# Retention: the first sequence's state one step later, and half of the first head's output weights split in step 0

## The chip, the cores and the metric

One NeuronCore of a Trainium2 chip runs the whole program. The metric is the device time of one execution in microseconds (us); the number compared is the median over several runs.

## The reference, cut to what matters

One step of a two-layer decoder for a prompt of 1024 tokens and 8 sample sequences of 8 tokens. The second layer is retention, and the change lies in it and in its output projection. Per head (4 of them, keys of 256, values of 512), with chunks of 128 tokens for the prompt and of 8 tokens for the samples:

```python
def step(S, inp):
    qc, kc, vc = inp
    o_inter = jnp.einsum('bhtk,bhkv->bhtv', qc, S) * q_decay
    scores = jnp.einsum('bhtk,bhsk->bhts', qc, kc) * intra_decay[None]
    o_intra = jnp.einsum('bhts,bhsv->bhtv', scores, vc)
    S_new = chunk_decay * S + jnp.einsum('bhsk,bhsv->bhkv', kc * k_decay, vc)
    return S_new, o_inter + o_intra
...
o = rms_norm(o).reshape(b, t, W_C) * jax.nn.silu(g.astype(f32))
return o.astype(h.dtype) @ w_out, s_new
```

A sample sequence is one such chunk: its output is computed from its old state `s0`, and its new state is `gamma^8 * s0 + k^T v` over its 8 tokens.

## The kernel before, in words

`retention_out` is the last stage of the program. Its main loop has `NSTEP = 32` steps, 4 heads by 8 prompt chunks, and every engine runs through the same steps by a program of its own; semaphores alone tie them together. Nothing is scheduled by a tool: the order of an engine's instructions is the order of the code.

In step n TensorE (the `block.tensor` program, `pe`) does, in this order:

1. the output of chunk n into `o`: three products of split operands (L2555), and from the second chunk of a head on the products with the running state (L2560), which wait for `state_done` of step n-1;
2. the update of the state into `u[0]`, `u[1]` (`product` at L2569); it waits until `s1_done` says that the sample state last put into `u` has been read;
3. `scores(n + 2)`, which needs that chunk's `q` and `k` in SBUF (`qk_in`);
4. `turn_out`, the transposes of the normed and gated output of step n-1;
5. in steps 2, 6, ... `sample_outputs`, the outputs of four sample sequences;
6. `sample_states(n - 1)`, the update of one sample sequence's state: two matmuls (L2505) into `u[0]` and `u[1]`;
7. `product_out`, the output projection of chunk n-2: 24 matmuls (L2528) with the weights `w_hi`, `w_lo`;
8. in steps 3, 7, ... the transposes of the sample outputs.

The sample keys and values are split into a high and a low part once, and then their rows are stacked by small SBUF to SBUF transfers, 8 partitions each: `stack(seq)` on ScalarE's queue writes three pieces of `v_stack`, `stack_keys(seq)` on GpSimd's queue three of `k_stack`. `sample_states(m)` waits for both (`stacked[m]`, `stacked_k[m]`). ScalarE stacks sequence n+1 in step n, GpSimd stacks sequence n in step n.

VectorE adds the state updates (L2772, L2775), gates (L2712), makes the low parts, writes the new sample states `s1` from `s0` and `u` (L2733), and adds the projection to the residual `y` (L2747). ScalarE rounds to the high parts and norms. The weights of a head's projection come as four rows `r` of 128 x 1024: `round_weights` on ScalarE makes `w_hi`, and `split_weights` makes `w_lo`, rows 0 and 2 on VectorE, rows 1 and 3 on GpSimd. For head 0 ScalarE does that in step 1, VectorE in step 1, GpSimd in step 3 of its own count.

SyncE (`sp`) issues the loads and stores on one queue, in the order of its code. In step n: `q`, `k` of chunk n+3, `v` of chunk n+3, the gate rows `g` of chunk n+3 (after `gated` of step n), then the store of the sample state n-1 (after `s1_done`), loads of later sample states into `s0`, and one tile of `y`. What stands behind a wait of this program is issued late.

Of the kernel before, what the change touches and what calls it, by code (L numbers as in the profile page):

```python
# [2174 lines left out]
def retention_out(nc, ahead, q_fm, k_fm, v_tm, g_tm, state_in, state_prompt, state_samples, mix_fm, consts, weight, x_of, y_of):  # L2175
# [6 lines left out]
    with nc.cleanup_on_exit(), ExitStack() as ctx:  # L2182
# [3 lines left out]
        NCH, J, R = TP // P, DK // P, DV // P  # L2186
        NGRP, SEQS = 2, NS // 2
        ROWS = SEQS * LS
        NSTEP = HC * NCH
# [87 lines left out]
        def outs_in(n):  # L2277

            return [] if n < 2 else [x for x in outs if x[0] == (n - 2) // NCH and x[1] == (n - 2) % NCH or
                                     (n - 2) % NCH == 6 and x == ((n - 2) // NCH, NT - 1)]  # L2280

        def qd_until(n):

            return n - n // NCH
# [14 lines left out]
        @block.sync  # L2299
        def _(sp):  # L2300
            def load_qk(n):
                h, c = divmod(n, NCH)
                for dst, src in ((q, q_cols), (k, k_cols)):
                    sp.dma_start(dst[:, n % NQ], src[h, :, c]).then_inc(qk_in[n % NQ], 16)

            def load_v(n):
                h, c = divmod(n, NCH)
                sp.dma_start(v[:, n % NV], v_rows[c * P:c * P + P, h]).then_inc(v_in[n % NV], 16)

            def load_g(n):  # L2310
                h, c = divmod(n, NCH)
                sp.dma_start(g[:, n % NV], g_rows[c * P:c * P + P, h]).then_inc(g_in[n % NV], 16)

            def load_s0(n):
                h, c = divmod(n, NCH)
                sp.dma_start(s0[c % SEQS][:], state_in[c, h].rearrange("(j k) v -> k j v", k=P)).then_inc(s0_in[c % SEQS], 16)

            def load_gs(h, grp):
                at = TP + grp * ROWS
                for s in range(SEQS):  # L2320
                    sp.dma_start(g_s[s * ROWS:(s + 1) * ROWS, grp, :], g_rows[at:at + ROWS, h]).then_inc(gs_in[grp], 16)

            def load_raw(h):
                for r in range(0 if h else 2, R):
                    sp.dma_start(raw_of(h, r), w_rows[:, h * R + r, :]).then_inc(raw_in[r], 16)

            def load_y(t):
                sp.dma_start(y[t][0:rows_of(t)], x_of(t)).then_inc(y_in[t], 16)

            def store_samples(m):  # L2330
                h, c = divmod(m, NCH)
                sp.wait_ge(s1_done, J * (m + 1))
                sp.dma_start(state_samples[c, h].rearrange("(j k) v -> k j v", k=P), s1[m % 2]).then_inc(s1_left[m % 2], 16)

            for x in ahead.left_tm:
                sp.wait_ge(x, LEFT)
            load_g(0)
            load_s0(0)
            load_g(1)
            for n in range(NSTEP):  # L2340
                h, c = divmod(n, NCH)
                if n + NQ < NSTEP:
                    sp.wait_ge(kt_done, n + 1)
                    sp.wait_ge(qd_done, qd_until(n))
                    load_qk(n + NQ)
                if n + NV < NSTEP:
                    sp.wait_ge(v_split, n + 1)
                    load_v(n + NV)
                    if n == 0:
                        load_raw(0)  # L2350
                        load_g(2)
                        for x in range(1, SEQS):
                            load_s0(x)
                        load_gs(0, 0)
                    sp.wait_ge(gated, unit_of["step", n] + 1)
                    load_g(n + NV)
                if c == NCH - 1:
                    sp.wait_ge(state_done, J * (n + 1))
                    sp.dma_start(state_prompt[h].rearrange("(j k) v -> k j v", k=P), state[:]).then_inc(state_left, 16)
                if n:  # L2360
                    store_samples(n - 1)
                    if (n - 1) % SEQS and n + 3 < NSTEP:
                        sp.wait_ge(o_done, unit_of["samples", (n - 1) // SEQS] + 1)
                        for x in (n + 2, n + 3) if (n - 1) % SEQS == 1 else (n + 3,):
                            load_s0(x)
                if 1 <= n < NCH:
                    if n == 4:
                        sp.wait_ge(w_split_d, R // 2)
                        sp.wait_ge(w_split_p, R // 2)
                    load_y(n - 1)  # L2370
                if n == 2:
                    load_gs(0, 1)
                if n == NCH - 1:
                    for seq in range(NS):
                        sp.wait_ge(stacked[seq], NSTACK)
                        sp.wait_ge(stacked_k[seq], NSTACK)
                    load_y(NT - 1)
                    load_y(NT - 2)
                if n % SEQS == 3 and h + 1 < HC:
                    sp.wait_ge(gated, unit_of["samples", n // SEQS] + 1)  # L2380
                    load_gs(h + 1, n // SEQS % NGRP)
                if c == NCH - 1 and h + 1 < HC:
                    sp.wait_ge(w_split_d, R // 2 * (h + 1))
                    sp.wait_ge(w_split_p, R // 2 * (h + 1))
                    load_raw(h + 1)
            store_samples(NSTEP - 1)
            for h, t in outs[-NT:]:
                sp.wait_ge(added, 2 * out_of[h, t] + 2)
                sp.dma_start(y_of(t), y[t][0:rows_of(t)]).then_inc(y_left, 16)
            sp.wait_ge(state_left, 16 * HC)  # L2390
            for i in range(2):
                sp.wait_ge(s1_left[i], 16 * NSTEP // 2)
            sp.wait_ge(y_left, 16 * NT)

        @block.gpsimd
        def _(pool):
            def split_weights(h):
                for r in range(1, R, 2):
                    pool.wait_ge(w_rounded, R * h + r + 1)
                    nc.gpsimd.tensor_tensor(w_lo[:, r, :], raw_of(h, r), w_hi[:, r, :].bitcast(F32), ALU.subtract).then_inc(w_split_p, 1)  # L2400

# [18 lines left out]
            for n in range(NSTEP):  # L2420
# [15 lines left out]
                        nc.gpsimd.tensor_copy(pick[:, s * LS:s * LS + LS], ident[:, at:at + LS]).then_inc(picked, 1)  # L2436
                elif n < NS:
                    stack_keys(n)
                if n == 3:
                    split_weights(0)  # L2440
                if n >= NCH and (n - 2) % NCH == 1 and n > NCH + 2:
                    split_weights((n - 3) // NCH)

# [1 line left out]
        def _(pe):  # L2445
# [44 lines left out]
                                       stop=(j == J - 1), skip_group_check=True, tile_position=(0, s * ROWS))  # L2490
                mm.then_inc(o_done, 1)

            def sample_states(m):


                h, c = divmod(m, NCH)
                if m < NCH:
                    pe.wait_ge(stacked[m], NSTACK)
                    pe.wait_ge(stacked_k[m], NSTACK)
                grp, rows = c // SEQS, slice(c % SEQS * ROWS, c % SEQS * ROWS + 3 * LS)  # L2500
                for j in range(J):
                    pe.wait_ge(state_done, J * min(m + 1, NSTEP - 1) + j + 1)
                    if m == NSTEP - 1:
                        pe.wait_ge(s1_done, J * (m - 1) + j + 1)
                    pe.matmul(u[j][:], k_stack[rows, grp, h, j], v_stack[rows, grp, h], start=True, stop=True,  # L2505
                              tile_position=(c % SEQS * ROWS, 0)).then_inc(us_done, 1)
# [40 lines left out]
            for n in range(NSTEP):  # L2547
# [16 lines left out]
                if n == 0:  # L2564
                    pe.wait_ge(first_scm, 1)
                for j in range(J):
                    if n >= 2:
                        pe.wait_ge(s1_done, J * (n - 2) + j + 1)
                    product(u[j][:], (kd_hi[:, i, j], kd_lo[:, i, j]), values).then_inc(u_done, 1)  # L2569

                if n + 2 < NSTEP:
# [7 lines left out]
                        pe.wait_ge(first_qd, 1)  # L2579
                    sample_outputs(h, c // SEQS)  # L2580

                if n:
                    sample_states(n - 1)
                for x in outs_in(n):
                    product_out(*x)
                for x in samples_before:
                    pe.wait_ge(picked, SEQS)
                    turn_out(x)
            sample_states(NSTEP - 1)
            for n in range(NSTEP, NSTEP + 2):  # L2590
                for x in turned_in(n) if n == NSTEP else ():
                    turn_out(x)
# [4 lines left out]
        def _(act):  # L2597
# [37 lines left out]
                act.wait_ge(tr_done, m + 1)  # L2635
                nc.scalar.copy(hi, src).then_inc(m_rounded, 1)

            def round_weights(h):
                for r in range(R):
                    if h and r < R - 1:  # L2640
                        act.wait_ge(w_used, (R - 1) * (h - 1) + r + 1)
                    elif h:
# [24 lines left out]
            for n in range(NSTEP):  # L2667
# [4 lines left out]
                    stack(n + 1)  # L2672
                for m in turned_in(n):
                    round_mix(m)
                if n == 1:
                    round_weights(0)
                if n % SEQS == 2:
                    norm(unit_of["samples", n // SEQS])
                if n > NCH and n % NCH == 1:
# [5 lines left out]
        def _(dve):  # L2685
# [30 lines left out]
                dve.wait_ge(m_rounded, m + 1)  # L2716
                dve.tensor_tensor(lo, src, hi.bitcast(F32), ALU.subtract).then_inc(m_split, 1)

            def split_weights(h):
                for r in range(0, R, 2):  # L2720
                    dve.wait_ge(w_rounded, R * h + r + 1)
                    dve.tensor_tensor(w_lo[:, r, :], raw_of(h, r), w_hi[:, r, :].bitcast(F32), ALU.subtract).then_inc(w_split_d, 1)

# [41 lines left out]
            for n in range(NSTEP):  # L2765
# [14 lines left out]
                step_before, *samples_before = turned_in(n) or [None]  # L2780
                if n:
                    split_mix(step_before)
                if n:
                    sample_states(n - 1)
                if n == 1:
                    split_weights(0)
                if n % SEQS == 2:
                    gate(unit_of["samples", n // SEQS])
                for x in outs_in(n):
                    add(*x)  # L2790
                for m in samples_before:
                    split_mix(m)
                if n > NCH and n % NCH == 1:
# [141 lines left out]
```

## Time and profile before

| | us |
|---|---|
| median of 3 runs | 2029.87 |
| the three runs | 2022.57, 2029.87, 2030.99 |
| the profiled execution, its own time | 2025.5 |
| its span, first to last instruction | 2023.5 |
| TensorE matmul busy, whole span | 1877.1 (93%) |
| VectorE, ScalarE, GpSimd busy | 852.8, 520.0, 594.4 |

The busy shares are averages over stages. The stage of this change begins near 1600 us and ends with the program; the profiled execution is 2.0 us longer than its span, and what happens in that stage is read from the rows further down. "PE" is TensorE's matmul side, "PEld" its weight load, "DVE" VectorE, "ACT" ScalarE, "POOL" GpSimd, "SP" SyncE; a "q" behind a name is that engine's DMA queue.

### The profile page before, as it was taken

Reading aid. Unit: us, or ns where it says so; the run is one execution under the profiler, and the core shown is the slowest. Engines: PE = TensorE matmul, PEld = TensorE weight load, DVE = VectorE, ACT = ScalarE, POOL = GpSimd, SP = SyncE. Lnnn points to the kernel's source line nnn. Section 1 sums busy time; section 2 is a strip of 40 time slices with the busy share of each in tenths; the row PEclk is TensorE's granted clock in tenths of the full one; section 3 lists DMA queues with packets and bytes.
Section 4 is the critical chain, followed back from the end, with each engine's and each line's share of the span. In section 5 each row is a group of like instructions: output and inputs, shape, how many; then the busy total and the mean of one; then the engine's idle time right before and its main releaser. Section 6 shows DMA issues by size and latency. Waiting matters only on the chain. (4 is left out here: it accounts for less than half of the span.)

```text
span 2023.5 us, 30854 instructions
## 1 busy us (share of the span) xinstructions
PE 1877.1 (93%) x11538; PEld 1511.4 (75%) x11538; DVE 852.8 (42%) x1474; ACT 520.0 (26%) x1133; POOL 594.4 (29%) x532
## 2 busy tenths in 40 slices
PE   6999999988887885789999999999999889999998
PEld 5788999974454553667899998888888657777776
DVE  3552000038788445874344442111000255656564
ACT  5210111047676432343310000000111232323231
POOL 3333222026666004313052222233330141313120
PEclk9999999989899897798999999999999989999999
DMA  4233224141330675345433223222324487665643
GB/s 154 78 107 107 99 103 139 50 141 46 118 115 27 207 224 192 115 133 175 132 122 90 86 86 101 89 91 93 101 95 128 124 226 249 193 199 155 203 136 141
DMA packets 209993, 261.58 MB, mean 129 GB/s; under 512 B 24260, under 2 KB 150660, under 8 KB 209604
## 3 DMA queue, kind: packets, MB, share of 16 engines
q1 hardware_dynamic: 154756, 201.50, 31.9%
q10 hardware_dynamic: 53104, 53.04, 8.0%
q0 software_dynamic: 2000, 5.25, 0.9%
q8 instruction: 86, 1.41, 0.3%
q14 instruction: 47, 0.39, 0.1%
HBM read 175.97 MB, written 81.40 MB: 127 GB/s over the span
## 5 line engine op out<-in xcount | busy, mean ns | idle before, releaser
L476 PE MATMUL odd_bank<-odd_w_hi,odd_h_hi 128*128 128x512 f32 x576 | 224.1, 389 | 0.0
L476 PE MATMUL odd_bank<-odd_w_lo,odd_h_hi 128*128 128x512 f32 x576 | 224.1, 389 | 0.0
L476 PE MATMUL odd_bank<-odd_w_hi,odd_h_lo 128*128 128x512 f32 x512 | 199.2, 389 | 0.0
L419 POOL CAST odd_w_hi<-ahead_raw 128x1024 fp32r<-128x1024 f32 x48 | 51.5, 1073 | 332.9 <-PE odd_bank L476 312.2
L476 PE MATMUL odd_bank<-odd_h_hi,odd_w_hi 128*128 128x362 f32 (+1 forms) x384 | 126.0, 328 | 1.8 <-POOL odd_w_lo L421 1.8
L476 PE MATMUL odd_bank<-odd_h_lo,odd_w_hi 128*128 128x362 f32 (+1 forms) x384 | 126.0, 328 | 0.0
L476 PE MATMUL even_bank<-even_h_hi,even_w_lo 128*128 128x362 f32 (+1 forms) x384 | 126.0, 328 | 0.0
L476 PE MATMUL even_bank<-even_h_hi,even_w_hi 128*128 128x362 f32 (+1 forms) x384 | 125.9, 328 | 0.0
L476 PE MATMUL even_bank<-even_h_lo,even_w_hi 128*128 128x362 f32 (+1 forms) x384 | 125.8, 328 | 0.0
L476 PE MATMUL odd_bank<-odd_h_hi,odd_w_lo 128*128 128x362 f32 (+1 forms) x384 | 125.0, 326 | 0.0
L476 PEld LDWEIGHTS odd_bank<-odd_w_lo,odd_h_hi 128*128 128x128 f32 x576 | 108.1, 188 | 22.4
L476 PEld LDWEIGHTS odd_bank<-odd_w_hi,odd_h_hi 128*128 128x128 f32 x576 | 108.1, 188 | 22.4
L476 PE MATMUL even_bank<-even_w_hi,even_h_hi 128*128 128x512 f32 x288 | 113.9, 395 | 5.0 <-DVE even_head_n L842 4.4
L421 POOL TENSOR_TENSOR odd_w_lo<-ahead_raw,odd_w_hi 128x1024 fp32r<-128x1024 f32 x48 | 115.9, 2414 | 3.8
L476 PE MATMUL even_bank<-even_w_lo,even_h_hi 128*128 128x512 f32 x288 | 113.0, 392 | 0.0
L476 PEld LDWEIGHTS odd_bank<-odd_w_hi,odd_h_lo 128*128 128x128 f32 x512 | 96.1, 188 | 20.0
L2528 PE MATMUL rt_y<-rt_w_hi,rt_m_hi 128*128 128x512 f32 x256 | 103.3, 404 | 0.0
L419 POOL CAST even_w_hi<-even_raw 128x1024 fp32r<-128x1024 f32 x32 | 33.6, 1050 | 232.3 <-PE even_bank L476 192.3
L476 PE MATMUL even_bank<-even_w_hi,even_h_lo 128*128 128x512 f32 x256 | 100.6, 393 | 0.0
L660 ACT ACT_TABLE_LOAD x2 | 2.6, 1283 | 380.3 <-PE odd_bank L476 380.3
L2528 PE MATMUL rt_y<-rt_w_hi,rt_m_lo 128*128 128x512 f32 x256 | 100.0, 391 | 0.0
L2528 PE MATMUL rt_y<-rt_w_lo,rt_m_hi 128*128 128x512 f32 x256 | 99.7, 390 | 0.0
(349 smaller groups left out, 4099.7 us busy)
## 6 DMA issues: line engine op xcount, KB each, us to landing
ahead_raw<-in_w_in_odd SPq DMA_DIRECT2D x48, 512.0 KB, 3.7
even_raw<-in_w_in_even SPq DMA_DIRECT2D x32, 512.0 KB, 3.9
k_page<-in_cache_k SPq DMA_DIRECT2D x64, 256.0 KB, 3.0
v_page<-in_cache_v SPq DMA_DIRECT2D x64, 256.0 KB, 3.0
rt_s<-in_state_ret SPq DMA_DIRECT2D x32, 512.0 KB, 5.4
v_tm<-odd_shared ACTq DMA_DIRECT2D x64, 128.0 KB, 1.9
g_tm<-odd_shared ACTq DMA_DIRECT2D x64, 128.0 KB, 1.9
first_place<-v_tm SPq DMA_DIRECT2D x32, 256.0 KB, 5.2
```

The source lines that it names most:

```text
L419: nc.gpsimd.tensor_copy(hi, r).then_inc(w_hi_done, 1)
L421: nc.gpsimd.tensor_tensor(lo, r, hi.bitcast(F32), ALU.subtract).then_inc(w_split, 1)
L476: mm = pe.matmul(out, stationary, moving, start=(j == 0), stop=(j == len(pairs) - 1))
L660: nc.scalar.activation(stage_tm[0:r, slot, :], src[0:r, :], ACT.Silu).then_inc(freed[0], 1)
L2528: mm = pe.matmul(yp[half][:], a[:, r, :], b[:, r, cols], start=(r == 0 and j == 0), stop=(r == R - 1 and j == len(ops) - 1))
```

## The change

A new table `states_in(n)` says whose sample state is computed in step n: none in steps 0 and 1, sequence 0 in step 2, sequences 1 and 2 in step 3, and from step 4 on sequence n-1 as before. TensorE's and VectorE's `sample_states` and SyncE's stores and `s0` loads follow it. In step 3 the second sequence comes behind `product_out`. The first head's weights are rounded and split in two halves: rows 0 and 1 in step 0 and rows 2 and 3 in step 1 on ScalarE, row 0 in step 0 and row 2 in step 1 on VectorE, row 1 in step 2 and row 3 in step 3 on GpSimd.

```diff
+        def states_in(n):
+            return {0: [], 1: [], 2: [0], 3: [1, 2]}.get(n, [n - 1])
...
-                if n:
-                    store_samples(n - 1)
-                    if (n - 1) % SEQS and n + 3 < NSTEP:
-                        sp.wait_ge(o_done, unit_of["samples", (n - 1) // SEQS] + 1)
-                        for x in (n + 2, n + 3) if (n - 1) % SEQS == 1 else (n + 3,):
+                for m in states_in(n):
+                    store_samples(m)
+                    if (m % SEQS or n == 2) and m + SEQS < NSTEP:
+                        sp.wait_ge(o_done, unit_of["samples", m // SEQS] + 1)
+                        for x in (m + SEQS - 1, m + SEQS) if m % SEQS == 1 and n > 3 else (m + SEQS,):
                             load_s0(x)
...
-                if n == 3:
-                    split_weights(0)
+                if n in (2, 3):
+                    split_weights(0, (2 * n - 3,))
...
-                    pe.wait_ge(state_done, J * min(m + 1, NSTEP - 1) + j + 1)
-                    if m == NSTEP - 1:
+                    pe.wait_ge(state_done, J * min(n, NSTEP - 1) + j + 1)
+                    if m != states_in(n)[0] or n == NSTEP:
                         pe.wait_ge(s1_done, J * (m - 1) + j + 1)
...
-                    if n >= 2:
-                        pe.wait_ge(s1_done, J * (n - 2) + j + 1)
+                    if n >= 3:
+                        pe.wait_ge(s1_done, J * states_in(n - 1)[-1] + j + 1)
...
-                if n:
-                    sample_states(n - 1)
+                behind, *more_behind = states_in(n) or [None]
+                if n >= 2:
+                    sample_states(behind, n)
                 for x in outs_in(n):
                     product_out(*x)
+                for x in more_behind:
+                    sample_states(x, n)
...
-                if n == 1:
-                    round_weights(0)
+                if n < 2:
+                    round_weights(0, (2 * n, 2 * n + 1))
...
-                if n:
-                    sample_states(n - 1)
-                if n == 1:
-                    split_weights(0)
+                behind, *more_behind = states_in(n) or [None]
+                if n >= 2:
+                    sample_states(behind)
+                if n < 2:
+                    split_weights(0, (2 * n,))
                 if n % SEQS == 2:
                     gate(unit_of["samples", n // SEQS])
                 for x in outs_in(n):
                     add(*x)
+                for m in more_behind:
+                    sample_states(m)
```

The order of the instructions, at three places. First TensorE at the border from step 1 to step 2 of the main loop; line numbers differ by a few between the two kernels. Before:

```order
L2459 MATMUL rt_sckt<-first_place 128x128 x2
L2461 MATMUL rt_sckt<-first_place 128x128 x2
L2472 MATMUL rt_tr<-first_place,rt_og 128x128 x4
L2505 MATMUL rt_u<-rt_v_stack,rt_k_stack 128x512 x2
L2451 MATMUL rt_o<-rt_v_hi,rt_scm_hi 128x512
```

and of the change:

```order
L2465 MATMUL rt_sckt<-first_place 128x128 x2
L2467 MATMUL rt_sckt<-first_place 128x128 x2
L2478 MATMUL rt_tr<-first_place,rt_og 128x128 x4
L2457 MATMUL rt_o<-rt_v_hi,rt_scm_hi 128x512
L2457 MATMUL rt_o<-rt_v_lo,rt_scm_hi 128x512
```

The two matmuls of the sample state, which need the stacked rows, no longer stand between the transposes of step 1 and the products of step 2.

Second VectorE over steps 0 and 1, from the low part of the scores of chunk 2 on. Before:

```order
L2701 TENSOR_TENSOR rt_scm_lo<-first_place,rt_scm_hi 128x128
L2775 SCALAR_TENSOR_TENSOR rt_state<-rt_state,rt_u 128x512 x2
L2712 SCALAR_TENSOR_TENSOR rt_og<-rt_o,rt_rs,rt_g 128x512
L2693 TENSOR_TENSOR first_place<-rt_sckt,first_place 128x128
L2698 SCALAR_TENSOR_TENSOR rt_kd_lo<-rt_sckt,ahead_k_dec,rt_kd_hi 128x256
L2701 TENSOR_TENSOR rt_scm_lo<-first_place,rt_scm_hi 128x128
L2717 TENSOR_TENSOR rt_m_lo<-rt_tr,rt_m_hi 128x512
L2733 SCALAR_TENSOR_TENSOR rt_s<-rt_s,rt_u 128x512 x2
L2722 TENSOR_TENSOR rt_w_lo<-ahead_raw,rt_w_hi 128x1024
L2722 TENSOR_TENSOR rt_w_lo<-rt_y,rt_w_hi 128x1024
```

and of the change:

```order
L2710 TENSOR_TENSOR rt_scm_lo<-first_place,rt_scm_hi 128x128
L2731 TENSOR_TENSOR rt_w_lo<-ahead_raw,rt_w_hi 128x1024
L2784 SCALAR_TENSOR_TENSOR rt_state<-rt_state,rt_u 128x512 x2
L2721 SCALAR_TENSOR_TENSOR rt_og<-rt_o,rt_rs,rt_g 128x512
L2702 TENSOR_TENSOR first_place<-rt_sckt,first_place 128x128
L2707 SCALAR_TENSOR_TENSOR rt_kd_lo<-rt_sckt,ahead_k_dec,rt_kd_hi 128x256
L2710 TENSOR_TENSOR rt_scm_lo<-first_place,rt_scm_hi 128x128
L2726 TENSOR_TENSOR rt_m_lo<-rt_tr,rt_m_hi 128x512
L2731 TENSOR_TENSOR rt_w_lo<-rt_y,rt_w_hi 128x1024
```

The first weight row's low part now stands ahead of the state update of step 1, and the sample state (L2733) is gone from step 1.

Third SyncE's queue from the `q` of chunk 4 (step 1) to the `q` of chunk 5 (step 2). Before:

```order
L2304 DMA first_place<-q_fm 128x256
L2304 DMA first_place<-k_fm 128x256
L2308 DMA first_place<-v_tm 128x512
L2312 DMA rt_g<-g_tm 128x512
L2333 DMA out_ret_sample<-rt_s 128x2x512
L2328 DMA rt_y<-y 128x1024
L2304 DMA first_place<-q_fm 128x256
```

and of the change:

```order
L2309 DMA first_place<-q_fm 128x256
L2309 DMA first_place<-k_fm 128x256
L2313 DMA first_place<-v_tm 128x512
L2317 DMA rt_g<-g_tm 128x512
L2333 DMA rt_y<-y 128x1024
L2309 DMA first_place<-q_fm 128x256
```

The store of the first sample state, which waits for `s1_done`, moves from step 1 to step 2, behind the loads of chunk 5.

## Rows read from the trace of the kernel before

**Rows 1.** The profile page's first line: span of the execution.

```profile
span 2023.5 us, 30854 instructions
```

**Rows 2.** What TensorE waited for, 1600 to 2023 us: total, times, longest.

```profile
PE rt_u L2505 <- issue: 7.7, 1, 7.7
PE rt_sckt L2459 <- PEq L219: 3.3, 1, 3.3
...
PE rt_tr L2472 <- DVE rt_ms L2717: 0.2, 1, 0.2
```

**Rows 3.** Windows: length, busy of PE, PEld, DVE, ACT, POOL, clock, DMA, GB/s.

```profile
1638.00:1658.00 20.00, 20.00 (x89) 15.14 (x90) 9.98 (x18) 4.37 (x13) 3.52 (x5) 1.00 0.72 199
...
1950.00:2000.00 50.00, 50.00 (x229) 35.67 (x228) 26.97 (x46) 11.77 (x34) 4.64 (x5) 1.00 0.30 98
```

**Rows 4.** TensorE's timeline, steps 1 and 2: start, length, group, [idle before].

```profile
1613.97 1.95 PE L2560 MATMUL rt_o<-rt_state,ahead_place 128*128 128x512 f32 x4 [0.58 <-DVE rt_state L2772]
1615.36 0.79 PE L2451 MATMUL rt_u<-rt_v_hi,rt_kd_hi 128*128 128x512 f32 x1
...
1617.15 0.61 PE L2459 MATMUL rt_sckt<-first_place 128*128 128x128 f32 x4
...
1617.81 0.60 PE L2472 MATMUL rt_tr<-first_place,rt_og 128*128 128x128 f32 x4
1626.12 1.19 PE L2505 MATMUL rt_u<-rt_v_stack,rt_k_stack 24*128 24x512 f32 x2 [7.71 <-issue]
1627.24 0.80 PE L2451 MATMUL rt_o<-rt_v_hi,rt_scm_hi 128*128 128x512 f32 x1
...
1628.69 2.90 PE L2560 MATMUL rt_o<-rt_state,ahead_place 128*128 128x512 f32 x4
1631.02 0.80 PE L2451 MATMUL rt_u<-rt_v_hi,rt_kd_hi 128*128 128x512 f32 x1
...
1633.70 0.71 PE L2459 MATMUL rt_sckt<-first_place 128*128 128x128 f32 x4 [0.71 <-DMA first_place<-k_fm]
...
1637.84 0.73 PE L2505 MATMUL rt_u<-rt_v_stack,rt_k_stack 24*128 24x512 f32 x2
1638.49 0.50 PE L2528 MATMUL rt_y<-rt_w_hi,rt_m_hi 128*128 128x512 f32 x1
```

**Rows 5.** DMA issues 1616 to 1620 us: count, KB each, us to landing.

```profile
first_place<-v_tm SPq DMA_DIRECT2D x1, 256.0 KB, 17.3
rt_v_stack<-rt_raw ACTq DMA_DIRECT2D x3, 64.0 KB
...
first_place<-k_fm SPq DMA_DIRECT2D x1, 128.0 KB, 17.0
```

**Rows 6.** SyncE's queue in time, steps 1 and 2.

```profile
1616.67 0.43 SPq L2304 DMA_DIRECT2D first_place<-k_fm  x1
...
1628.31 0.40 SPq L2333 DMA_DIRECT2D out_ret_sample<-rt_s  x1
```

**Rows 7.** ScalarE, VectorE and GpSimd in time, steps 0 to 2.

```profile
1618.16 0.60 ACT L2622 ACTIVATE rt_og<-rt_o 128x512 f32<-128x512 f32 x1 [1.93 <-issue]
...
1624.13 1.99 ACT L2645 CAST rt_w_hi<-ahead_raw 128x1024 fp32r<-128x1024 f32 x2
...
1617.27 1.27 DVE L2775 SCALAR_TENSOR_TENSOR rt_state<-rt_state,rt_u 128x512 f32<-128x512 f32 x2
...
1628.20 1.47 DVE L2722 TENSOR_TENSOR rt_w_lo<-ahead_raw,rt_w_hi 128x1024 fp32r<-128x1024 f32 x1
...
1618.82 1.26 POOL L2417 TENSOR_TENSOR rt_v_lo<-first_place,rt_v_hi 128x512 fp32r<-128x512 f32 x1
```

**Rows 8.** Windows of 2 us, columns as in rows 3.

```profile
1620.00:1622.00 2.00, 0.00 (x0) 0.00 (x0) 1.16 (x4) 0.66 (x2) 1.99 (x5) 0.62 1.13 260
...
1626.00:1628.00 2.00, 1.88 (x4) 1.16 (x5) 1.00 (x2) 2.00 (x3) 1.79 (x1) 0.50 0.61 167
...
1630.00:1632.00 2.00, 2.00 (x6) 1.01 (x5) 2.00 (x1) 0.38 (x1) 1.88 (x1) 0.82 1.00 273
```

More of the change, by code:

```diff
@@ L2396, in _, with split_weights @@
         def _(pool):
-            def split_weights(h):
-                for r in range(1, R, 2):
+            def split_weights(h, rows=(1, 3)):
+                for r in rows:
                     pool.wait_ge(w_rounded, R * h + r + 1)
@@ L2491, in sample_outputs, with sample_states @@
                 mm.then_inc(o_done, 1)
-            def sample_states(m):
+            def sample_states(m, n):
                 h, c = divmod(m, NCH)
@@ L2588, in _ @@
                     turn_out(x)
-            sample_states(NSTEP - 1)
+            sample_states(NSTEP - 1, NSTEP)
             for n in range(NSTEP, NSTEP + 2):
@@ L2636, in round_mix, with round_weights @@
                 nc.scalar.copy(hi, src).then_inc(m_rounded, 1)
-            def round_weights(h):
-                for r in range(R):
+            def round_weights(h, rows=range(R)):
+                for r in rows:
                     if h and r < R - 1:
@@ L2717, in split_mix, with split_weights @@
                 dve.tensor_tensor(lo, src, hi.bitcast(F32), ALU.subtract).then_inc(m_split, 1)
-            def split_weights(h):
-                for r in range(0, R, 2):
+            def split_weights(h, rows=(0, 2)):
+                for r in rows:
                     dve.wait_ge(w_rounded, R * h + r + 1)
```

## The prediction

> **What bounds the kernel now.** I read four views, from the coarse to the fine. The list of waits over the last stage first: from 1600 us on TensorE waits once for long, 7.7 us, at the first sample state's matmul (L2505); the next in the list is the stage's start-up, 3.3, and the last 0.2 us [rows 2]. Then the windows: from 1638 us on TensorE is busy for the whole of each stretch, 20.00 of 20 us and still 50.00 of 50 at 1950, at the full clock [rows 3]. So the end of the program is the moment at which the steady state begins plus a fixed amount of TensorE work. I take as that moment the first `product_out`, at 1638.49 us [rows 4]. Whatever the change does after it, on engines that have half their time free, costs or gives nothing as long as TensorE stays full. All of the question is what stands between 1617.81 and 1638.49.
>
> Third, TensorE's timeline there [rows 4]. Its transposes of step 1 begin at 1617.81. Then it is idle for 7.71 us and resumes at 1626.12 with the sample state. The running state that this matmul also waits for was ready at 1617.27 + 1.27 = 1618.54 [rows 7], so what is late are the stacked rows, which come by small transfers. From 1626.12 it works up to the scores of chunk 4, and there it waits again, 0.71 us, for `k` of chunk 4, and starts at 1633.70. The fourth view is the DMA list: `k` was issued at 1616.67 [rows 6] and took 17.0 us [rows 5], so it landed at 1633.7. `v` of the same chunk took 17.3 us. This is the point of the case: the second wait is short only because the first one stands before it. Both belong to one backlog of transfers, issued at the head of the stage, that drains until about 1634.
>
> **The change part by part.**
>
> *The sample state leaves step 1.* TensorE goes from the transposes of step 1 straight to the products of step 2. They need the low part of `v`, ready at 1618.82 + 1.26 = 1620.08 [rows 7]. The state products behind them need the running state of step 1. That one now stands behind a new instruction on VectorE: the low part of weight row 0, which needs ScalarE's rounding of it. ScalarE does two rows in 1.99 us and begins at 1618.16, where the norm of step 1 began [rows 7]; the first row is done at about 1619.2. VectorE's part takes 1.47, which gives 1620.7, and the state update another 1.27: 1622.0 in place of 1618.54. The three products ahead take 1.45 us even at the half clock (1627.24 to 1628.69) [rows 4], from 1620.1 to 1621.5, so TensorE waits half a microsecond here. The state products take 2.33 us at the half clock (1628.69 to 1631.02) or 1.39 at the full one (1613.97 to 1615.36), the products into `u` 1.79 at the full clock (1615.36 to 1617.15) [rows 4]; at the half clock I take 1.7 times that, 3.0. So TensorE comes to the scores of chunk 4 between 1622.0 + 1.39 + 1.79 = 1625.2 and 1622.0 + 2.33 + 3.0 = 1627.3, 6.4 to 8.5 us earlier than now.
>
> *What is late next.* Exactly `k` of chunk 4. SyncE issues it ahead of everything that the change moves: the order shows `q`, `k`, `v`, `g` of that step in the same places, and only behind them the first tile of `y` and the loads of chunk 5 in place of the store of the sample state. So it is issued at 1616.67 as before, and its 17 us are queueing behind what was issued earlier. Two things change around it. ScalarE's stacking of sequence 2 moves behind the two roundings, some 2 us later, and GpSimd's stacking of sequence 3 behind a weight split; that takes traffic out of the way. And `y` (512 KB) with `q`, `k`, `v` of chunk 5 (512 KB) come in at about 1623 in place of 1628; that adds traffic, but later in the same queue. No row of before shows how the landing answers to either. From below: if the stackings that moved had been all that held it, it would come about 2 us earlier, by their shift; if all of the backlog went, the wait would vanish and only the 6.4 to 8.5 us above bound the gain. From above: 1 MB of new traffic at what such stretches move (260 GB/s in the row at 1620, 273 at 1630 [rows 8]) is about 3.8 us, if `k` had to wait for all of it. I take 1 us earlier, 1632.7, nearer to no change than to either end, because the issue time and everything ahead of it in its own queue stay.
>
> The Trainium skill bears on this (DMA: Bandwidth & Descriptors, section on queues, rings and completion order): each of the 16 DMA engines takes the descriptors of one queue in ring order and goes round the queues by packet; and its section on the semaphore increment by 16 says that a copy of 8 partitions runs on 8 engines alone, the lowest-numbered. By that rule the 8-partition stackings load half of the engines, and `k` ends with the slower half; the trace agrees in that the mean DMA share is 0.61 from 1626 to 1628 while `k` is still outstanding [rows 8]. By ring order alone the landing would stay at 1633.7, and the sum below would be 1 us larger, 2028.0 in place of 2027.0, inside the forecast's own case.
>
> *The clock.* Now TensorE is idle from 1618.4 to 1626.1, and its granted clock falls to half, 1.2 GHz, in the row at 1620 (0.62) and is there still in the row at 1626 (0.50). In the row from 1630 to 1632 it is 0.82, so half for 2 * 0.18 / 0.5 = 0.7 us and full, 2.4 GHz, from about 1630.7, 4.6 us after work resumed [rows 8]. Today these 4.6 us cost nothing, since the 0.71 us of waiting for `k` follows. After the change the long idle time, about 1626 to 1632.7, stands directly before the piece that nothing absorbs: scores, transposes, sample outputs, sample state, up to the projection. At the full clock that piece takes 1638.49 - 1633.70 = 4.79 us. At the half clock the sample state took 1.12 (1626.12 to 1627.24) against 0.65 (1637.84 to 1638.49), and the state products 2.33 against 1.39, a ratio of 1.7 in both [rows 4]. 4.6 us at that ratio do the work of 2.7, a loss of 1.9 us. From below the loss is nothing, should the burst at 1620 to 1626 keep the clock up; from above 2.4, were the whole piece slow and it recovered no sooner than the piece ends.
>
> *The sample state that is still owed.* Before, states 0 and 1 are done ahead of the first projection, after it only state 0 is; the third one in step 3 is the missing one. It now falls in the full stretch: 0.65 us [rows 4].
>
> *Weights, `s0` loads, stores.* The weight rows are all ready before the projection at 1638 in both orders: row 3 is rounded by about 1629 and split in 2 to 3.5 us on GpSimd. In step 3 the state of sequence 2 comes behind the projection on TensorE and VectorE, and the `u` products of step 4 wait for VectorE to read it. Between them TensorE has 8 small transposes and the output products, over 2.5 us, against two VectorE instructions; that is hidden, and if it were not, it would cost at most 1 us once. Loads of `s0` go out one step apart and are needed three steps later. All of this I cost at nothing.
>
> **The sum:** -1.0 (landing) + 1.9 (clock) + 0.65 (owed state) = +1.5 us. The profiled execution took 2025.5 us, so 2027.0; its span of 2023.5 [rows 1] grows by the same. The median shown is 4.4 us above that execution, and from it the sum would be 2031.4. The three runs lie from 2022.57 to 2030.99, so I set the forecast between the two, 2029.0. Since 0.5% is 10 us and that is about what a measurement of this kernel can tell from no change, the forecast is no change.
>
> **Rivals.**
>
> *The stall moves to `k` of chunk 4 and the time stays* (forecast), 0.78. By the bounds of the landing and the clock, -2.0 + 0 + 0.65 = -1.4 to 0 + 2.4 + 0.65 = +3.1.
>
> *The gain is kept.* Loads land much earlier since the stackings are spread, and TensorE finds `k` there at 1625.2 to 1627.3. For it: the stackings share the DMA engines with `k`, and ACT's three of 64 KB each stand in the same list [rows 5]. Against it: most of what is ahead of `k` in its own queue is not touched. Price: -8.5 + 0.65 = -7.9 to -6.4 + 0.65 = -5.8 us; from a base of 2029.0 - 1.5 = 2027.5 that is 2019.6 to 2021.7. Even whole it is 0.39%. Chance 0.14, with the part-way cases.
>
> *The loads collide and it gets slower.* `y` and chunk 5 enter the DMA engines five microseconds earlier and take bandwidth from `k`: landing at 1637.5, and +3.8 + 2.4 + 0.65 = +6.9 us, 2034.4. It speaks for it that the DMA share is near 1 in the windows at 1620 and 1630 [rows 8], against it that they stand behind `k`. It would be slower by over 0.5% only if the landing came 7.1 us later than now, past 1640.8. Chance 0.08.
>
> **How the numbers follow.** No case by itself crosses 10 us in either direction; what crosses it is the scatter of the runs, 8.4 us over three. So faster 0.05, within 0.5% 0.90, slower 0.05. The range takes the lowest run less 1.4 and the highest plus 4.5, part of the way into the two rivals: 2021.0 to 2035.5.
>
> **What would show it.** Right, if in the new profile the 7.7 us at L2505 are gone and a wait of 5 to 8 us stands before the scores of chunk 4, released by the DMA of `k_fm`, with the clock at half behind it, and the first projection begins between 1637 and 1642. The step on the landing is wrong if that wait is under 4 us or `k` lands before 1630; the step on the clock is wrong if the granted clock is full through the sample outputs. The forecast as a whole is wrong if TensorE has gaps after the first projection, which I costed at nothing.

## The result and the profile after

The change is slower: its median over 9 runs is 2034.22 us (2031.01 to 2039.52), that of the kernel before over 9 runs beside it 2029.87 (2022.57 to 2038.1); the ratio is 1.0042, 95% interval 1.0024 to 1.0060. That is 5 to 12 us, clear of zero, and the interval reaches over the 0.5% that I had called no change. The ratio compares runs of the same rounds; the two medians by themselves are 4.4 us apart. The profiled execution took 2031.74 us, with a span of 2030.0.

```profile
span 2030.0 us, 30855 instructions
```

The list of waits of TensorE over the last stage of the change (total, times, longest):

```profile
PE rt_sckt L2465 <- DMA first_place<-k_fm: 11.3, 2, 10.7
PE rt_sckt L2465 <- PEq L219: 3.3, 1, 3.3
...
PE rt_o L2457 <- issue: 1.8, 1, 1.8
PE rt_o L2566 <- DVE rt_state L2784: 1.4, 1, 1.4
```

The 7.7 us at the sample state of [rows 2] are gone, and 10.7 us before the scores of chunk 4 have come. TensorE's timeline of the change shows what follows them, beside [rows 4]:

```profile
1613.78 0.60 PE L2478 MATMUL rt_tr<-first_place,rt_og 128*128 128x128 f32 x4
1616.14 0.47 PE L2457 MATMUL rt_o<-rt_v_hi,rt_scm_hi 128*128 128x512 f32 x1 [1.77 <-issue]
...
1618.47 1.95 PE L2566 MATMUL rt_o<-rt_state,ahead_place 128*128 128x512 f32 x4 [1.40 <-DVE rt_state L2784]
...
1632.54 1.23 PE L2465 MATMUL rt_sckt<-first_place 128*128 128x128 f32 x4 [10.74 <-DMA first_place<-k_fm]
...
1634.97 1.93 PE L2491 MATMUL rt_o<-first_place,rt_scm_s 32*32 32x512 f32 x8
1636.84 3.54 PE L2495 MATMUL rt_o<-rt_s,ahead_place 128*32 128x512 f32 x16
1640.30 0.73 PE L2511 MATMUL rt_u<-rt_v_stack,rt_k_stack 24*128 24x512 f32 x2
1640.96 0.50 PE L2534 MATMUL rt_y<-rt_w_hi,rt_m_hi 128*128 128x512 f32 x1
```

The absolute times of two executions can't be set against each other here: this stage began at 1598.23 us in the change's profile and at 1601.67 in that of before, by chance of what lies ahead of it. From here on every time of this stage is counted from the stage's first matmul. So counted, the scores of chunk 4 begin at 1632.54 - 1598.23 = 34.3 in place of 32.0, the first projection (the `product_out` of step 2) at 42.7 in place of 36.8, and from the projection to the end it is 2030.0 - 1640.96 = 389.0 in place of 2023.5 - 1638.49 = 385.0. The three differences, 2.3 (wait), 3.6 (from the scores to the projection, 8.4 in place of 4.8) and 4.0 (after it), make 9.8 us.

The windows of the change (length, busy of PE, PEld, DVE, ACT, POOL, clock, DMA, GB/s) show the clock of the middle piece, and a second dip:

```profile
1624.00:1626.00 2.00, 0.00 (x0) 0.00 (x0) 2.00 (x4) 1.30 (x5) 1.71 (x1) 1.00 1.16 233
1626.00:1628.00 2.00, 0.00 (x0) 0.00 (x0) 0.38 (x1) 0.00 (x0) 0.73 (x1) 0.62 0.78 101
1632.00:1636.00 4.00, 3.46 (x18) 2.30 (x18) 0.97 (x3) 1.28 (x3) 3.15 (x5) 0.50 0.37 129
1636.00:1640.00 4.00, 4.00 (x24) 0.60 (x16) 0.69 (x1) 0.58 (x1) 0.33 (x1) 0.50 0.44 75
1640.00:1642.00 2.00, 2.00 (x11) 1.16 (x8) 1.09 (x2) 1.19 (x4) 0.00 (x0) 0.97 0.00 0
...
1660.00:1664.00 4.00, 4.00 (x10) 2.16 (x9) 1.19 (x3) 0.27 (x1) 0.00 (x0) 0.58 0.93 316
```

TensorE had been idle since 1621.8, and the clock fell to half in the row that begins at 1626 (0.62). Work resumed at 1632.54, and the clock was at 1.2 GHz (0.50) until about 1640.1 (0.97 in the row that begins at 1640), 7.6 us; in [rows 8] it had come back 4.6 us after work resumed. It fell to half once more in step 3, from 1660.6 on, with TensorE busy throughout; there the same state products that took 1.88 us one step earlier took 3.39:

```profile
1647.22 1.88 PE L2566 MATMUL rt_o<-rt_state,ahead_place 128*128 128x512 f32 x4
...
1658.15 1.06 PE L2511 MATMUL rt_u<-rt_v_stack,rt_k_stack 24*128 24x512 f32 x2 [0.23 <-DVE ahead_place L2742]
1659.14 1.08 PE L2480 MATMUL rt_tr<-rt_pick,rt_og 128*128 128x32 f32 x8
...
1660.99 3.39 PE L2566 MATMUL rt_o<-rt_state,ahead_place 128*128 128x512 f32 x4
```

On SyncE's queue `k` of chunk 4 goes out as early in the stage as before (14.7 us after its first matmul, before 15.0), and the new traffic is there, 5 us and more ahead of [rows 6]:

```profile
1612.90 1.09 SPq L2309 DMA_DIRECT2D first_place<-k_fm  x1
...
1619.39 0.43 SPq L2333 DMA_DIRECT2D rt_y<-y  x1
1619.92 0.38 SPq L2309 DMA_DIRECT2D first_place<-q_fm  x1
```

### The profile page after: what moved, and what is told of

The parts are those of the page before. It is cut to its first block and busy times, and to the rows that moved or that the text cites. A ratio compares the mean times of both kernels' runs of the same rounds, so it can differ in the third digit from the quotient of the medians.

```text
span 2030.0 us, 30855 instructions
## 1 busy us (share of the span) xinstructions
PE 1875.3 (92%) x11538; PEld 1508.7 (74%) x11538; DVE 852.7 (42%) x1474; ACT 519.8 (26%) x1133; POOL 592.8 (29%) x532
```

## The experiments

All ratios are to the kernel before, timed in the same rounds, with 95% intervals. "One run" means that the kernel was only profiled. The table gives, from one profile of each, the start of the scores of chunk 4, the start of the first projection (both from the stage's first matmul), the time from that projection to the end of the program, and the sum of the last two, in us (each rounded by itself).

| run | ratio | scores 4 | projection | to the end | sum |
|---|---|---|---|---|---|
| the kernel before | 1 | 32.0 | 36.8 | 385.0 | 421.9 |
| before_again | one run | 31.6 | 36.4 | 385.0 | 421.5 |
| the change | 1.0042 (1.0024 to 1.0060) | 34.3 | 42.7 | 389.0 | 431.7 |
| change_again | 1.0034 (1.0014 to 1.0055) | 34.5 | 42.8 | 388.1 | 430.9 |
| states_only | 1.0033 (1.0012 to 1.0055) | 32.7 | 41.7 | 388.9 | 430.6 |
| weights_only | 0.9987 (0.9970 to 1.0005) | 31.4 | 36.2 | 385.0 | 421.2 |
| hold_loads | 1.0015 (0.9995 to 1.0035) | 29.6 | 38.6 | 388.4 | 427.0 |
| pair_in_2 | 1.0039 (1.0020 to 1.0058) | 32.6 | 41.7 | 387.9 | 429.5 |
| warm | 1.0014 (0.9995 to 1.0033) | 34.0 | 38.7 | 389.1 | 427.8 |
| hold_warm | 0.9992 (0.9967 to 1.0017) | 29.4 | 34.2 | 386.5 | 420.7 |
| hold_before | one run | 33.1 | 42.1 | 388.1 | 430.2 |
| k_first | 0.9985 (0.9963 to 1.0007) | 25.4 | 30.1 | 387.1 | 417.2 |
| k_first_again | 0.9983 (0.9959 to 1.0007) | 23.5 | 38.0 | 389.4 | 427.5 |
| k_first_before | 0.9975 (0.9952 to 0.9997) | 29.8 | 36.9 | 385.6 | 422.4 |
| k_first_old_weights | 1.0000 (0.9970 to 1.0030) | 21.8 | 32.7 | 389.0 | 421.7 |
| k_first_pair | 0.9969 (0.9945 to 0.9992) | 26.4 | 31.1 | 386.4 | 417.4 |
| k_first_pair_again | 1.0001 (0.9979 to 1.0024) | 23.6 | 29.7 | 390.7 | 420.4 |

**1. Which half of the change costs.** states_only keeps the states' new place and takes the weights back to where they were; weights_only is the reverse.

```diff
 # states_only, against the change
...
-                if n < 2:
-                    round_weights(0, (2 * n, 2 * n + 1))
+                if n == 1:
+                    round_weights(0)
...
```

> The sample states move as in the change (none in step 1, state 0 in step 2, 1 and 2 in step 3); the weights are rounded and split as before the change. Theory A, the whole cost hangs on the moved states: the long wait moves to k of chunk 4, the clock is half behind it, and step 3 has its dip of the clock; the time is that of the change, 4 to 9 us over the kernel before. Theory B, the weights' new place costs: VectorE's state update of step 1 comes at 1618.5 in place of 1622 of before's count, and the cost falls to 0 to 3 us.

> Only the weights are rounded and split in two halves; the sample states stay where they were. Theory A: nothing changes within 2 us, since TensorE still waits for the stacked rows until long after the weights are ready. Theory B: 3 us or more slower, since VectorE's state update of step 1 and ScalarE's norm and stacking stand behind the weights.

Measured: states_only 1.0033, weights_only 0.9987 with 1 inside its interval. In states_only the wait before the scores is 10.5 us and the piece behind it 9.0. Theory A holds in what costs: it is the states' new place alone. Its dip of the clock in step 3 did not come; the clock was at half for the first 3.7 us of the projection instead (see 4).

**2. Why `k` lands late.** hold_loads keeps the new loads out of the way of `k`.

```diff
                 if 1 <= n < NCH:
+                    if n == 1:
+                        sp.wait_ge(qk_in[4 % NQ], 64)
                     if n == 4:
```

> The change, and SyncE waits in step 1 for the landing of q and k of chunk 4 before it issues the first tile of y and the loads of chunk 5. Theory C, the 1 MB issued 5 to 9 us earlier than before is what made k land 2.3 us later in the stage: k lands about 2 us earlier and the time falls by 2 us. Theory D, k is held by what was issued ahead of it alone: the landing and the time stay within 1 us of the change.

The scores begin at 29.6 in place of 34.3, 4.7 us earlier, and the stage is 4.7 us shorter; the ratio falls from 1.0042 to 1.0015, with intervals that overlap. Theory C is right for the change, by more than it said: in the five profiles that issue the 1 MB early and `k` at its usual place, `k` landed at 32.6 to 34.5, in the two that hold the 1 MB back (this and hold_warm) at 29.3 and 29.6, 3 to 5 us earlier. TensorE's timeline of hold_loads also shows that this did not pay in full:

```profile
1630.26 1.23 PE L2467 MATMUL rt_sckt<-first_place 128*128 128x128 f32 x4 [5.59 <-DMA first_place<-k_fm]
1634.56 3.64 PE L2497 MATMUL rt_o<-rt_s,ahead_place 128*32 128x512 f32 x16
1639.28 0.80 PE L2536 MATMUL rt_y<-rt_w_hi,rt_m_hi 128*128 128x512 f32 x1
```

`k` is there 2.4 us earlier than in the kernel before, and the projection still begins 1.8 us later, at half clock: from scores to projection it is 9.0 us.

**3. The clock.** warm fills the wait with work whose result is overwritten.

```diff
+                if n == 2:
+                    pe.wait_ge(first_ks, HC)
+                    pe.wait_ge(w_rounded, 1)
+                    for x in range(46):
+                        pe.matmul(yp[0][:], w_hi[:, 0, 0:P], w_hi[:, 0, 0:512], start=True, stop=True)
                 if n + 2 < NSTEP:
                     scores(n + 2)
```

> The change, with 46 extra matmuls of 128x512 on TensorE in step 2 ahead of the scores of chunk 4; their result is overwritten by the projection, so they fill the wait for k and nothing else. Theory F, the clock: what follows the wait was slow only because TensorE had been idle. Then the granted clock stays full, from the scores of chunk 4 to the projection it is 4.8 us in place of 8.4, and the time is 3 to 5 us under the change's. Rival: the piece is slow for another reason (late DVE or DMA), and the time stays or rises by what the fillers overrun, up to 1 us.

The windows of warm and its timeline, where the scores begin at 1628.23:

```profile
1624.00:1628.00 4.00, 4.00 (x19) 3.30 (x18) 0.00 (x0) 0.00 (x0) 0.74 (x1) 1.00 0.58 147
1628.00:1634.00 6.00, 6.00 (x43) 2.98 (x42) 3.21 (x6) 2.95 (x8) 2.77 (x4) 1.00 0.52 117
```

```profile
1628.23 0.61 PE L2465 MATMUL rt_sckt<-first_place 128*128 128x128 f32 x4
...
1630.41 1.92 PE L2495 MATMUL rt_o<-rt_s,ahead_place 128*32 128x512 f32 x16
1632.92 0.50 PE L2534 MATMUL rt_y<-rt_w_hi,rt_m_hi 128*128 128x512 f32 x1
```

The clock stays full, and the piece is 4.7 us in place of 8.4. The scores begin as late as in the change (34.0), here because of the fillers: `k` went out at 1609.30 and took 17.8 us, so it was there at 32.9, and the fillers overran it by 1.1 us. Nothing else was altered, so those 3.7 us of the piece are the clock's, and the clock's fall the idle time's. The stage is 3.9 us shorter than the change's (427.8 against 431.7), inside the 3 to 5 expected. The Trainium skill states it from the other side (TensorE: Matmul & The Clock Gate, part 1): "the default state is throttled, and activity releases the throttle"; these rows agree. hold_warm puts both together, with 26 extra matmuls.

> Both: SyncE holds the first tile of y and the loads of chunk 5 back until k of chunk 4 has landed, and 26 extra matmuls of 128x512, overwritten later, fill the wait. If traffic and clock together are the cause, the first projection begins 34 to 35 us after the stage's first matmul (before 36.8, change 42.7), and the time is 1 to 2 us under the kernel before. If the two do not add up, it stays over it.

The projection begins at 34.2, as expected, and the whole stage is 1.2 us shorter than before; the ratio, 0.9992, can't tell that from no change. Traffic and clock add up: the projection comes 42.7 - 34.2 = 8.5 us earlier than in the change, against 4.1 (hold_loads) and 4.0 (warm) singly.

**4. What comes after the projection.** pair_in_2 puts sample state 1 behind the projection of step 2, so that step 3 has one state, ahead of its projection.

```diff
-            return {0: [], 1: [], 2: [0], 3: [1, 2]}.get(n, [n - 1])
+            return {0: [], 1: [], 2: [0, 1]}.get(n, [n - 1])
```

> The change, but sample state 1 is computed at the end of step 2, behind the projection, and state 2 alone in step 3 ahead of the projection. Theory E, the half clock of 3.4 us that the change shows in step 3 comes from the two sample matmuls and the eight narrow transposes standing together: it is gone, and the time from the first projection to the end is 1.7 to 2.4 us shorter than with the change. Rival: the dip comes with any sample state behind a projection, and stays, then in step 2.

The dip of step 3 is gone, but it is gone as well in the profiles of states_only, hold_loads, hold_warm, k_first and k_first_again, which keep the pair; it stands in those of the change, change_again, warm and k_first_old_weights. So the pair is not enough by itself to bring it, and k_first_pair_again, without the pair in step 3, has a half clock in step 2 after a wait of 2.3 us for VectorE. The time to the end fell by 1.1 us only, not by the 1.7 to 2.4 expected, since in this run the clock was still at half for the first 3.6 us of the projection.

The time from one projection to the next says more. From that of step 3 to that of step 4 it is 12.1 us in the kernel before, in before_again and in weights_only; 13.6 in the five profiles with the pair and without the dip, hold_warm (1642.80 to 1656.41) among them; and 15.3 in the change (1652.18 to 1667.44), change_again and warm, 16.1 in k_first_old_weights. So the moved state costs 1.5 us and the dip 1.7. From the projection of step 2 to that of step 3 it is 11.2 us before and in the change, and 13.0 or 13.1 in states_only, hold_loads and k_first_again, where the clock comes back only some 4 us into the projection: 1.8 us for that. In pair_in_2 the two together are 13.8 + 12.5 = 26.3 us, against 11.2 + 12.1 = 23.3 before; less the 1.8 of the clock, its moved state costs 1.2. What was expected of it, the dip of 1.7 us gone, is so in this profile, but it can't be put down to the pair.

**5. Is the difference in the landing the change's.** The change and the kernel before were profiled once more, and the kernel before with the wait of experiment 2.

> The change itself once more, beside the next three. If the account by stages holds, its first projection begins 41 to 43 us into the stage and it is 0.25 to 0.5% over the kernel before. If the profile of it was an outlier, the landing of k and with it the stage are within 1 us of the kernel before.

> The kernel before, profiled once more. k of chunk 4 landed 32.0 us into the stage there, 34.3 and 34.5 in two profiles of the change. If that difference is the change's, it lands at 31 to 33 again and the first projection begins at 36 to 37.5; if it is scatter of the transfers, it can as well land at 34.

> The kernel before, with the first tile of y and the loads of chunk 5 held back until k of chunk 4 has landed. If traffic issued behind k slows it also here, k lands at 29 to 31 us of the stage and the 0.7 us of waiting for it is gone; if not, it stays at 32.

The repeats agree with the first profiles to 0.4 us (34.5 and 31.6). hold_before went against its expectation: `k` came at 33.1, later than in the kernel before, with none of the 1 MB behind it. So the landing also scatters by a microsecond or so. Over all profiles that issue `k` at its usual place and hold nothing back it is 31.4 to 32.0 in the old order (three) and 32.6 to 34.5 in the new one (five); with hold_before at 33.1 the two overlap, and the difference of 2.3 us is that of one pair of profiles. What is firm is that `k` came no earlier in any of the five than in those three. hold_before also shows what a late landing does. Its timeline and windows:

```profile
1630.54 1.22 PE L2461 MATMUL rt_sckt<-first_place 128*128 128x128 f32 x4 [2.66 <-DMA first_place<-k_fm]
1634.83 3.64 PE L2491 MATMUL rt_o<-rt_s,ahead_place 128*32 128x512 f32 x16
1639.55 0.80 PE L2530 MATMUL rt_y<-rt_w_hi,rt_m_hi 128*128 128x512 f32 x1
```

```profile
1630.00:1636.00 6.00, 5.46 (x26) 2.70 (x30) 2.30 (x5) 1.86 (x4) 3.49 (x5) 0.50 0.77 222
1636.00:1640.00 4.00, 4.00 (x15) 1.15 (x8) 0.66 (x2) 1.19 (x4) 0.00 (x0) 0.50 0.38 111
```

A wait of 2.7 us in front of the scores, in the old order, was followed by 13 us of work at half clock; `k` was 1.1 us later than in [rows 4] and the projection 5.3 us later. The kernel before, with waits of 0.7 and 0.9 us at this place, stays on the good side of that.

**6. Taking the cause away.** k_first issues `q` and `k` of chunk 4 ahead of three sample states.

```diff
-                if n + NQ < NSTEP:
+                if n + NQ < NSTEP and n != 1:
                     sp.wait_ge(kt_done, n + 1)
...
                         load_g(2)
+                        sp.wait_ge(kt_done, 2)
+                        sp.wait_ge(qd_done, qd_until(1))
+                        load_qk(4)
                         for x in range(1, SEQS):
                             load_s0(x)
```

> The change, but SyncE issues q and k of chunk 4 in step 0 ahead of the loads of three sample states. Theory G, k is late only because it queues behind what was issued ahead of it: it lands before TensorE asks for it, the 10.7 us wait is gone, the next late thing are the sample states or v of chunk 4, and the first projection begins 28 to 32 us into the stage, 5 to 8 us earlier than in the kernel before. Rival: the wait only moves on, to the sample states that now land later, and the gain is under 2 us.

> The change with q and k of chunk 4 issued ahead of three sample states, once more. If the first profile (first projection at 30.1 us of the stage, 4.7 us less from the stage's start to the end than in the kernel before) is what it does, the time is 0.1 to 0.3% under the kernel before and 0.4 to 0.6% under the change. If that profile was luck, it lies with the change.

> The kernel before with the same earlier issue of q and k of chunk 4. TensorE still waits 7.7 us for the stacked rows in step 1, and only the 0.7 us in front of the scores can go: the time is within 1 us of the kernel before. If it gains more, the early issue is worth something without the moved states.

> As k_first, but the weights are rounded and split as before the change. Theory H, the weight half of the change pays only once the stall is gone: the projection then waits for the last weight row, which GpSimd splits in 2 to 3 us behind the first, and begins 2 to 4 us later than with k_first (30.1 us of the stage). Rival: the weights are early enough in either order, the projection begins no later, or up to 1.4 us earlier, because VectorE's state update of step 1 is not held up.

> As k_first, and sample state 1 behind the projection of step 2 in place of step 3. The two sample states of step 3 cost 0.4 us of waiting on each other and stand with the narrow transposes; without that, the time from the first projection to the end is 0.3 to 0.8 us shorter than with k_first, or, if the dip of the clock that two of the profiles show comes from there, never shows that dip. It is expected within 0.1% of k_first.

> The change with k of chunk 4 issued early and sample state 1 behind the projection of step 2, once more. If its 0.3% under the kernel before is real, the ratio is again 0.995 to 0.999; if the sample states land late, TensorE waits up to 6 us for them and the clock is half behind it, and the ratio is 1.000.

In the first profile theory G is borne out whole: no wait at the scores, projection at 30.1. In the second the wait is at the sample outputs, for a sample state's load that now stands behind `k`, and the clock is half behind it. TensorE's timeline of k_first_again:

```profile
1626.55 1.93 PE L2494 MATMUL rt_o<-first_place,rt_scm_s 32*32 32x512 f32 x8 [6.28 <-DMA rt_s<-in_state_ret]
1628.41 3.64 PE L2498 MATMUL rt_o<-rt_s,ahead_place 128*32 128x512 f32 x16
1633.13 0.80 PE L2537 MATMUL rt_y<-rt_w_hi,rt_m_hi 128*128 128x512 f32 x1
```

So the rival is right as well: the wait moves on in some executions, and the stage took 417.2 us in one profile and 427.5 in the other. Timed, all versions with the early `k` lie 0 to 0.3% under the kernel before, 0.3 to 0.7% under the change, and cannot be told from each other. k_first_pair came out at 0.9969, with a time to the end 0.7 us shorter than k_first's, as expected; its repeat came out at 1.0001, with a wait of 2.3 us for VectorE behind the projection and 390.7 us to the end. So its gain over the kernel before is not established; nor is that of k_first_before (0.9975), whose profile shows no gain (422.4 against 421.9) and for which I have no explanation but scatter. Theory H, that the early weights pay once the stall is gone, stays open: k_first_old_weights begins its projection 2.6 us later than k_first, but its waits are 2.7 us for a sample state and the clock behind that, none for the weights.

## Why the prediction was wrong

It said no change, +1.5 us by the sum; measured were +5 to +12, by the stage's profile +9.8. The median of 2034.22 does lie in the stated range of 2021.0 to 2035.5, but that range was as wide as the scatter of single runs and says nothing for the sum. Two of the signs I gave failed too: the wait before the scores was 10.7 us, not 5 to 8, and the first projection began at 42.7 us of the stage, which is 1644.4 in the count of [rows 4], not 1637 to 1642.

**The path was right.** The 7.7 us at L2505 went, VectorE's state update was late by the weight row (a wait of 1.4 us; I had half a microsecond: the state update came when I said, 20.2 us into the stage, but the three products ahead of the wait ran earlier and at the full clock), and the stall moved in front of the scores of chunk 4, released by `k_fm`. TensorE stood ready at 34.3 - 10.7 = 23.6 us of the stage, 8.4 before the scores begin in [rows 4], inside the 6.4 to 8.5 I gave. weights_only confirms that the weights cost nothing that can be measured (0.9987, with 1 in the interval).

**Step "what is late next": "I take 1 us earlier, 1632.7".** Wrong in sign: +2.3 and, in the repeat, +2.9 against the second profile of before; over all five profiles with the early loads +0.6 to +2.5 on 32.0, and never earlier. I let the unchanged issue time and the order within `k`'s own queue decide and treated 1 MB issued behind it as nearly harmless; hold_loads and hold_warm show that it cost 3 to 5 us. My upper bound, 3.8 us over the old landing, held. The rule of the Trainium skill that I weighed (DMA: Bandwidth & Descriptors, queues and rings, ring order in each queue) is about the order in which an engine takes descriptors, and would have left the landing at 32.0; the rows of hold_loads and of the change don't agree with reading it as protection of an earlier transfer's time. By which path the later loads slow `k` no run here shows. I also gave the lowest-numbered engines for all copies of 8 partitions. The Trainium skill (DMA: Bandwidth & Descriptors, section on the increment by 16) says so of copies from SyncE's and ScalarE's queues; for GpSimd's, half of the stackings here, it has a first engine that moves on from copy to copy. No run here shows which engines they took.

**Step "the clock": 1.9 us, bounded by 2.4.** Mis-sized: 3.6, and 3.7 in warm. I took the 4.6 us of recovery from [rows 8], where TensorE had wide products to do. In the change it had transposes and the sample outputs, and the clock came back after 7.6 us; in hold_loads and hold_before it was half through the entire piece and some 4 us into the projection. That the narrow work is the reason is not shown. The bound was wrong in itself: 2.4 is what half of 4.79 makes, but a piece of 4.79 us that runs whole at my ratio of 1.7 takes 8.1, 3.4 us more. The ratio was too low as well: the whole piece at half clock took 9.0 us in place of 4.8 (hold_loads), 1.9 times as long, because the sample outputs nearly double (1.92 to 3.64), and my 1.7 came from two other products.

**Step "all of this I cost at nothing" and "the sample state that is still owed": 0.65 us.** Mis-sized: 4.0 in this profile. 1.5 is the moved state with its wait of 0.2 us on VectorE (hold_warm), 1.7 the dip of the clock in step 3 (3.4 us at half), and the rest mostly a wait of 0.6 us for another chunk's `k` some 90 us later, which states_only, warm and k_first_again have too and which change_again and hold_loads have not (change_again is 388.1 us to the end in place of 389.0); I can't lay that one at the change's door.

The terms in place of mine: +2.3 + 3.6 + 4.0 = +9.8 against -1.0 + 1.9 + 0.65 = +1.5. I also priced the rival of the colliding loads at +6.9 and gave it 0.08. By direction it is what happened; the landing was priced too high (3.8 for 2.3), the clock and the owed state too low. And I took the scatter of single runs, 8 us, for the limit of what a median can tell; the interval over nine runs a side was 7 us wide and did not hold zero.

## What to carry to other kernels

A wait that is removed from the busiest engine is worth only what the next late transfer leaves of it: look up when that one lands, and count what the earlier progress itself puts on the queues ahead of it. Ask also where the idle time stands. 7.7 us of idleness cost nothing extra in front of work that ended in another wait; 2.7 to 10.7 us of it cost 3.5 to 4.2 us in front of work that nothing absorbs, and in some profiles 1.8 more behind that. For a stretch of 40 us in a program of 2000, whose start lay 18 us apart over these seventeen profiles, times counted from the stage's first instruction show in a few profiles what nine timed runs a side only just resolve; one profile is not enough, since the landings and the clock differ between two profiles of one kernel (k_first and its repeat).

## What I had not expected of the hardware

- The granted clock can stay at 1.2 GHz for 8 to 13 us of nearly uninterrupted work: in hold_before it is 0.50 from 1630 to 1640 with TensorE busy 9.5 of 10 us, and it comes back only 4 us into the projection.
- A wait of 2.7 us was followed by that; waits of 0.9 and 2.0 us at the same place (before_again, weights_only) were not.
- A load of 128 KB (`k` of chunk 4) can take 16 to 20 us to land (issued at 1612.90, there at 1632.5 in the change) while the DMA engines move 101 to 273 GB/s in the rows shown, and 1 MB issued behind it went with 3 to 5 us of that; in hold_before, without it, the landing was late all the same.
